# PEER stage of a hybrid encoder: one operand of VectorE's one-hots and sums moved into PSUM, gathered steps regrouped

## The reference

```python
q = (xt @ w_pq).reshape(T, 8, 2, 128)
s1 = einsum('thd,hnd->thn', q[:, :, 0], k1)      # 128 keys each
s2 = einsum('thd,hnd->thn', q[:, :, 1], k2)
t1, i1 = top_k(s1, 16); t2, i2 = top_k(s2, 16)
ts, ci = top_k(t1[..., :, None] + t2[..., None, :], 16)
e = i1[ci // 16] * 128 + i2[ci % 16]              # one of 16384 experts
g = softmax(ts)
act = gelu(einsum('td,thkd->thk', xt, u_tab[e]))
out = einsum('thk,thkd->td', g * act, v_tab[e])
```

## Time and profile before

| | us |
|---|---|
| median of 3 runs | 2577.13 |
| lowest, highest | 2574.62, 2577.2 |
| the profiled execution's own time | 2580.62 |
| its span, from first to last instruction | 2578.8 |

### The profile page before, as it was taken

The page is one execution under the profiler, slowest core; times in us unless marked ns, Lnnn a source line. Parts: engine busy times, 40 slices in busy tenths (PEclk is TensorE's granted clock), DMA queues, the critical chain, the costliest instruction groups (busy, mean ns, idle before and its releaser), DMA issues.

```text
span 2578.8 us, 29605 instructions
## 1 busy us (share of the span) xinstructions
PE 2331.2 (90%) x11005; PEld 1786.0 (69%) x11005; DVE 1622.4 (63%) x2696; ACT 666.8 (26%) x1419; POOL 964.2 (37%) x552
## 2 busy tenths in 40 slices
PE   6699999899879999997897988888879999999996
PEld 6699977665457978997897888888834444444442
DVE  2376654444543222999889799999835555555555
ACT  2143520133322212242333344434300110001011
POOL 8455455400004424264656665555411111111110
PEclk9899999955689999998998999999989999999998
DMA  6323233300133213164666777777799999999994
GB/s 237 105 99 109 98 107 124 104 20 17 33 94 139 66 33 128 42 233 139 226 229 203 235 252 282 281 271 280 268 361 371 374 381 378 386 377 383 383 376 180
DMA packets 192546, 541.94 MB, mean 210 GB/s; under 512 B 17057, under 2 KB 116194, under 8 KB 158882
## 3 DMA queue, kind: packets, MB, share of 16 engines
q1 hardware_dynamic: 113024, 243.30, 27.5%
q0 software_dynamic: 27776, 201.40, 20.4%
q10 hardware_dynamic: 51618, 95.52, 10.3%
HBM read 472.18 MB, written 67.67 MB: 209 GB/s over the span
## 4 chain that ended last, share of the span: by engine, by line
PE 61%; DVE 27%; issue 5%; ACT 2%; DMA 2%; POOL 2%; SPq 1%; ACTq 0%; DVEq 0%; POOLq 0%
PE ps L949 24%; PE ps L579 17%; PE ps L904 6%; PE ps L696 5%; DVE yg L1887 3%; PE ps L729 3%; DVE hot L2030 3%; DVE ring L1879 2%; DVE hot L2032 2%; PE ps L558 2%; PE ps L779 2%; PE ps L733 1%; DMA ge<-ge_scratch 1%; SPq L446 1%; DVE xn L1529 1%
## 5 line engine op out<-in xcount | busy, mean ns | idle before, releaser
L949 PE MATMUL ps<-vraw,gf 128*128 128x512 f32 x1536 | 665.1, 596 | 19.0 <-DVE gf L2046 11.4
L949 PEld LDWEIGHTS ps<-vraw,gf 128*128 128x128 f32 x1536 | 293.0, 191 | 390.6 <-issue 372.6
L505 POOL DMA_INDIRECT ring<-uv,place_of x192 | 228.0, 1188 | 789.6 <-DVE yg L1887 783.1
L904 PE MATMUL ps<-actH,uH 128*128 128x384 f32 x1024 | 355.7, 347 | 57.9 <-POOL uL L497 45.5
L497 POOL TENSOR_TENSOR uL<-uraw,uH 128x1024 fp32r<-128x1024 f32 x128 | 332.6, 2616 | 100.6 <-ACT uH L1389 99.3
L487 POOL TENSOR_SCALAR wH<-raw 128x1024 fp32r<-128x1024 f32 x112 | 120.5, 1094 | 653.7 <-PE ps L579 500.7
L904 PE MATMUL ps<-actL,uH 128*128 128x384 f32 x1024 | 349.1, 341 | 0.0
L904 PE MATMUL ps<-actH,uL 128*128 128x384 f32 x1024 | 348.4, 340 | 0.0
L1887 DVE SCALAR_TENSOR_TENSOR yg<-ring,coef,yg 128x1024 f32<-128x1024 f32 x192 | 280.0, 1458 | 36.6 <-ACT coef L1442 36.5
L1879 DVE SCALAR_TENSOR_TENSOR ring<-ring,xn 128x1024 f32<-128x1024 f32 x192 | 267.5, 1394 | 43.4 <-DMA ring<-uv,place_of 42.7
L579 PE MATMUL ps<-actH,wH 128*128 128x288 f32 (+1 forms) x960 | 288.2, 300 | 6.8 <-DVE actL L1546 6.8
(11 more groups left out here) (286 smaller groups left out, 3298.2 us busy)
## 6 DMA issues: line engine op xcount, KB each, us to landing
uraw<-wu SPq DMA_DIRECT2D x128, 512.0 KB, 4.4
vraw<-wv SPq DMA_DIRECT2D x128, 512.0 KB, 7.9
raw<-wts SPq DMA_DIRECT2D x56, 1024.0 KB, 4.9
ge_scratch<-ge ACTq DMA_DIRECT2D x128, 192.0 KB, 4.2
c_scratch<-cst ACTq DMA_DIRECT2D x12, 2048.0 KB, 8.1
cg<-c_scratch SPq DMA_DIRECT2D x32, 768.0 KB, 13.5
ge<-ge_scratch SPq DMA_DIRECT2D x128, 192.0 KB, 8.7
xres<-x ACTq DMA_DIRECT2D x2, 2048.0 KB, 12.1
```

The costliest lines, as they stand in the source:

```text
L505: pool.indirect_dma_start(out=ring[:, s % RING, :], out_offset=None, in_=a["uv"], in_offset=bass.IndirectOffsetOnAxis(ap=place_of[:, s:s + ...
L904: mm = pe.matmul(bank(b, TD), lhs, rhs, start=k == 0 and w == 0, stop=k == KT - 1 and w == 2)
L949: mm = pe.matmul(bank(2 * i + half), gf[:, q % GF_RING, i * P:(i + 1) * P], vraw[:, q % V_RING, half * CHUNK:(half + 1) * CHUNK], start=q ...
```

## The change

- **PSUM operands.** ACT copies iota into PSUM (`iota_ps`, bank 3) and the transposed gates stay there as `gates_ps` (bank 3), where PE's transposes put them; chosenT keeps only the two keys. So each of the three one-hot instructions has one operand in SBUF and one in PSUM. Tile 4's sums (`yg4`) lie in banks 4 and 5 during the up stage; ACT copies them to yg[:, 0] once the 64 accumulates are done, and PE's first down waits before it writes those banks (`yg4_copied`). The one-hots' products have three banks (C_BANKS) instead of four.
- **Steps.** All 64 early steps, which are those of tile 4, stand behind the 48 groups, hot_of_step(s) = s * 48 // 64; none in the ranking. `accumulate(s - 2)` follows `dot(s)` (LAG = 2), in the up stage and in the down stage. `gather(s)` is issued behind the `low` that is four ups after the group of step s - 2. ACT's coefficients of a group's steps stand before the copy_gates of the next group.
- **Places.** GATES_AT 13 to 16, EXPD_AT 54 to 42, TURN_AT 60 to 48, EXP3_AT 78 to 56, HOT_AT 75 to 54: the groups are spread over 73 ups instead of 52.

```diff
-PICKS_AT, GATES_AT, EXP4_AT, EXPD_AT, TURN_AT, EXP3_AT, HOT_AT, HOT_TO = 5, 13, 5, 54, 60, 78, 75, 127
-RANK_STEPS = 8
-RANKED = 3 * RANK_STEPS
-EARLY_STEPS = 64
+PICKS_AT, GATES_AT, EXP4_AT, EXPD_AT, TURN_AT, EXP3_AT, HOT_AT, HOT_TO = 5, 16, 5, 42, 48, 56, 54, 127
+EARLY_STEPS = STEPS4
+LAG = 2
...
 def hot_of_step(s):
-    return (s - RANKED) * HOTS // (EARLY_STEPS - RANKED)
+    return s * HOTS // EARLY_STEPS
...
-    chosenT = nc.alloc_sbuf_tensor_at("chosenT", [P, 3, TD], F32, offset=chosen_at)
+    chosenT = nc.alloc_sbuf_tensor_at("chosenT", [P, 2, TD], F32, offset=chosen_at)
...
+    iota_ps = ps[:, 3 * BANK + TD:4 * BANK]
+    gates_ps = ps[:, 3 * BANK:3 * BANK + TD]
+    yg4 = ps[:, 4 * BANK:6 * BANK]
+    C_BANKS = 3
...
-            while issued >= RING and step_place(issued - RING) + 4 <= n:
+            while RING <= issued < EARLY_STEPS and hot_place(hot_of_step(issued - LAG)) // 2 + 4 <= n:
                 gather(issued)
                 issued += 1
...
                 for s in range(3):
-                    mm = pe.transpose(ps[:, i * BANK + s * P:i * BANK + (s + 1) * P], chosen[:, i, s, :], ident[:, :])
+                    at = i * BANK + s * P if s < 2 else 3 * BANK + i * P
+                    mm = pe.transpose(ps[:, at:at + P], chosen[:, i, s, :], ident[:, :])
...
-                if q >= 4:
-                    pe.wait_ge(c_copied, q - 3)
+                if q >= C_BANKS:
+                    pe.wait_ge(c_copied, q - C_BANKS + 1)
...
+                if q == 0 and i == DENSE - 1:
+                    pe.wait_ge(yg4_copied, 1)
...
+            act.wait_ge(iota_in, 16)
+            act.activation(iota_ps, iota[:, :], ACT.Copy).then_inc(iota_copied, 1)
...
                     if hot_place(g) == h:
+                        for s in range(EARLY_STEPS):
+                            if hot_of_step(s) == g - 1:
+                                coefficient(s)
                         copy_gates(g)
-                        for s in range(RANKED, EARLY_STEPS):
-                            if hot_of_step(s) == g:
-                                coefficient(s)
...
+        act.wait_ge(acc_done, EARLY_STEPS)
+        act.activation(yg[:, 0, :], yg4, ACT.Copy).then_inc(yg4_copied, 1)
...
-            ve.scalar_tensor_tensor(yg[:, y_at, :], ring[:, s % RING, D:2 * D], coef[:, s:s + 1], yg[:, y_at, :],
-                                    ALU.mult, ALU.add).then_inc(acc_done, 1)
+            y = yg4 if s < STEPS4 else yg[:, 1, :]
+            ve.scalar_tensor_tensor(y, ring[:, s % RING, D:2 * D], coef[:, s:s + 1], y, ALU.mult, ALU.add)\
+              .then_inc(acc_done, 1)
...
-            dot(steps[0])
-            if steps[0]:
-                accumulate(steps[0] - 1)
+            s = steps[0]
+            if s < STEPS:
+                dot(s)
+            if s >= LAG:
+                accumulate(s - LAG)
...
-            rank(i, 0, PK_HEADS, full_work, gathered)
+            rank(i, 0, PK_HEADS, full_work, nothing)
...
-            ve.tensor_tensor(hot1[:, g % 2], iota[:, :].unsqueeze(1).broadcast_to(shape),
+            ve.tensor_tensor(hot1[:, g % 2], iota_ps.unsqueeze(1).broadcast_to(shape),
                              chosenT[:, 0, now].unsqueeze(2).broadcast_to(shape), ALU.is_equal)
-            step.done(ve.tensor_tensor(hot2[:, g % 2], iota[:, :].unsqueeze(1).broadcast_to(shape),
+            step.done(ve.tensor_tensor(hot2[:, g % 2], iota_ps.unsqueeze(1).broadcast_to(shape),
                                        chosenT[:, 1, now].unsqueeze(2).broadcast_to(shape), ALU.is_equal))
             ve.tensor_tensor(hot2[:, g % 2], hot2[:, g % 2],
-                             chosenT[:, 2, now].unsqueeze(2).broadcast_to(shape), ALU.mult).then_inc(hot_ready, 1)
+                             gates_ps[:, now].unsqueeze(2).broadcast_to(shape), ALU.mult).then_inc(hot_ready, 1)
...
+        while steps[0] < EARLY_STEPS + LAG:
+            accumulate(steps[0] - LAG)
+            steps[0] += 1
+        steps[0] = EARLY_STEPS
         for q in range(NKEYS):
             weigh(q)
             if steps[0] < STEPS:
-                gathered()
-        accumulate(STEPS - 1)
+                dot(steps[0])
+            if steps[0] >= EARLY_STEPS + LAG:
+                accumulate(steps[0] - LAG)
+            steps[0] += 1
+        for s in range(steps[0] - LAG, STEPS):
+            accumulate(s)
```

More of the change, by code:

```diff
@@ L388, in encoder_layer @@
         dot_ready acted_ready coef_ready acc_done gates_ready tile3_ready fold_ready folded
-        x2_in y_ready taken_up ss_in""".split()
+        x2_in y_ready taken_up ss_in iota_copied yg4_copied""".split()
     (const_in, gain_in, gain_used, memx_in, x_in, ssq_clear, ssq_ready, var_ready, std_ready, xn_ready, acth_done,
@@ L397, in encoder_layer @@
      dot_ready, acted_ready, coef_ready, acc_done, gates_ready, tile3_ready, fold_ready, folded,
-     x2_in, y_ready, taken_up, ss_in) = [S(name) for name in names]
+     x2_in, y_ready, taken_up, ss_in, iota_copied, yg4_copied) = [S(name) for name in names]
     ck_in = [S(f"ck_in{j}") for j in range(2)]
@@ L922, in c_tokens @@
                 q = 2 * g + half
-                if q >= 4:
-                    pe.wait_ge(c_copied, q - 3)
+                if q >= C_BANKS:
+                    pe.wait_ge(c_copied, q - C_BANKS + 1)
                 for t in range(4):
-                    at = (q % 4) * BANK + t * P
+                    at = (q % C_BANKS) * BANK + t * P
                     mm = pe.matmul(ps[:, at:at + P], hot1[:, g % 2, 4 * half + t, :], hot2[:, g % 2, 4 * half + t, :],
@@ L1414, in copy_choices @@
             act.wait_ge(chT_ready, DENSE)
+            act.wait_ge(iota_in, 16)
+            act.activation(iota_ps, iota[:, :], ACT.Copy).then_inc(iota_copied, 1)
             for i in range(DENSE):
                 act.activation(chosenT[:, :, i * P:(i + 1) * P],
-                               ps[:, i * BANK:i * BANK + 3 * P].rearrange("p (s t) -> p s t", s=3),
+                               ps[:, i * BANK:i * BANK + 2 * P].rearrange("p (s t) -> p s t", s=2),
                                ACT.Copy).then_inc(chT_copied, 1)
@@ L1428, in copy_gates @@
                 act.activation(cst[s][:, :, at + 4 * half:at + 4 * half + 4],
-                               bank(q % 4).rearrange("p (t e) -> p e t", t=4), ACT.Copy).then_inc(c_copied, 1)
+                               bank(q % C_BANKS).rearrange("p (t e) -> p e t", t=4), ACT.Copy).then_inc(c_copied, 1)
             if g % 4 == 3:
@@ L1464, in _ @@
                 exps(2 + DENSE, chosen[:, DENSE, 2, :])
-            for s in range(RANKED):
-                if step_place(s) + 1 == n:
-                    coefficient(s)
+        for s in range(EARLY_STEPS):
+            if hot_of_step(s) == HOTS - 1:
+                coefficient(s)
+        act.wait_ge(acc_done, EARLY_STEPS)
+        act.activation(yg[:, 0, :], yg4, ACT.Copy).then_inc(yg4_copied, 1)
         for s in range(EARLY_STEPS, STEPS):
@@ L1868, in best_of @@
             step.done(ins)
-        def row_of(s):
-            return (0, 0) if s < STEPS4 else (1, 1)
         def dot(s):
@@ L1876, in dot @@
                 ve.wait_ge(rows_in, 16)
-            x_at, _ = row_of(s)
+            x_at = 0 if s < STEPS4 else 1
             row = ring[:, s % RING, 0:D]
@@ L1993, in _ @@
         ve.sem_inc(gates_ready, 1)
-        step.done(ve.memset(yg[:, :, :], 0.0))
+        ve.memset(yg4, 0.0)
+        step.done(ve.memset(yg[:, 1, :], 0.0))
         step.done(ve.tensor_tensor(fold[:, :], ident[:, 0:NS_TOK], ident[:, NS_TOK:P], ALU.add))
@@ L2007, in _, with gates_at_first @@
         turn = [0]
-        def gathered_and_gates():
+        def gates_at_first():
             if turn[0] == 0:
@@ L2012, in gathered_and_gates @@
             turn[0] += 1
-            gathered()
         ve.wait_ge(ss_in, 16)
-        rank(DENSE, 0, PK_HEADS, full_work, gathered_and_gates)
+        rank(DENSE, 0, PK_HEADS, full_work, gates_at_first)
         expert_places(3, place_of[:, STEPS4:STEPS])
@@ L2020, in _ @@
         ve.wait_ge(chT_copied, DENSE)
+        ve.wait_ge(iota_copied, 1)
         for g in range(HOTS):
```

1 line of the change is left out of this document (removed).

## The result

The changed kernel takes **2619.51 us** (median of 4 runs, 2618.52 to 2624.7), the kernel before took 2577.16 beside it (2574.62 to 2577.28): ratio 1.0171, 95% interval 1.0153 to 1.0188. By that ratio it is 44 us slower (42 between the two medians); I had forecast +3. The profiled spans, 2622.9 and 2578.8, differ by 44.1 as well.

What follows compares the result with a forecast made beforehand. DVE was taken to bound the one-hot stage and PE the down stage. The terms, -3 to the end of the up stage and +6 in the down stage, gave +3 on 2580.6: 2584 us, or 2581 beside the median; range 2535 to 2620.

Steps and rivals of the forecast that it cites:

- rival 3: Down stage becomes bound by gathers, slots freed one step later: 2610 at landings of 8.2 us, 2668 at 9.1; chance 0.08.
- First one-hot: End of the ranking stage: 24 gathered steps leave it, 1482 - 126 = 1356 us, with 8 us either way.
- PSUM operands: DVE's one-hots and accumulates: no wait for POOL; accumulate that reads and writes PSUM taken at 1.2 us, 2.4 at most.
- Rival 4: One PSUM operand still waits for POOL, or writing PSUM is dear: +45 us, kernel 2625; chance 0.04.
- One-hot stage: First one-hot to end of up stage: chain of gathers makes it 513 us against 390 before, ending at 1869.
- landing: Gathers in the one-hot stage: median 6.7 us, 0.7 off for shorter issue, 1.2 on for long ones, 7.2.
- The third group and the clock's loss: One-hot stage, cycle of three groups: 8.1 us for the third group plus 2 us for PE's clock, sum 31.6.
- Clock: One-hot stage: behind waits of 4 to 5 us PE's clock is granted at 1.2 GHz, costing 2 us a cycle.
- Down stage: Sums two behind free a gather's slot one step later: +6 us, between 0 and 90, near the lower end.
- at 7.7 the loop is even: Down stage: with landings of 7.7 us, two steps hold landing, dot and accumulate within the 10.3 us PE needs.
- what was to show it: Signs: one-hots near 1.2 us, L927 waiting some 90, up stage ending near 1870, PE busy throughout the down stage.
- The issue row: Issue of gathers on POOL in the one-hot stage: 1.69 us of a landing, 0.95 at the shortest; 0.7 taken off.

Runs made afterwards that it cites:

- e8: The kernel before with the sums of the down stage two steps behind instead of one: 2607.24 us, ratio 1.0098.
- e1: The kernel before with the PSUM operands and sums and three banks alone, schedule as before: 2502.64 us, ratio 0.9709 to the kernel before.
- e2: The changed kernel with operands of one-hots and sums back in SBUF, its schedule kept: 2656.14 us, ratio 1.0319 to the kernel before.

## Why the prediction was wrong

What it said of the up stage held: the one-hot stage gives back what the ranking stage gains, because one-hots stand behind gathers and PE waits for them. In the down stage it was not the forecast that came true but its rival 3, which had a chance of 0.08. Two terms of the sum were too small: the one-hot stage by 25 us (513, 538) and the down stage by 28 (+6, +34), the larger part of the 41 us between +3 and +44.

- **First one-hot**: 1356 forecast, 1344.9 measured. 11 us in its favour, a little outside the 8 allowed. 7 of the 11 are not of the change: the ranking's first instruction starts at 1015.0 instead of 1022.3, and it started at 1016.4 in e8 too, whose program up to there is that of the kernel before. From it to the first one-hot 459.7 us became 329.8: 130 less, where 126 were forecast. The gathered steps account for 124 of them, 87 of work and 37 of waits. The ranking's own instructions came out 7 us shorter (325.6 to 318.7), within the 8 that the prediction allowed: L1934's 16.2 us became 2.9 (L1939) and L1917's 15.0 became 3.5 (L1922), while L1959's six went from 13.8 to 24.2 (L1964).
- **PSUM operands**: 1.2 us taken, 1.22 and 1.28 measured. Rival 4 is out.
- **One-hot stage**: 513 forecast, 538 measured. For 15 of the 16 gathers that are placed one group ahead and whose wait reached PE (the first, which landed in 12.4 us, left out) the traces give step by step: group to issue 7.60 us (forecast 7.6); landing **9.14** (7.2); dot, accumulate, three one-hots 6.1 (6.7); from group to group 22.9 (21.5). The third group and the clock's loss, 8.1 + 2.0 forecast, came to 10.4, as a cycle of three groups takes 33.3 us in the mean of the whole stage. So 33.3 x 47/3 = 522 instead of 495; this and not the shape of the chain is the 25 us. The step that failed is "median 6.7 in this stage ..., and I take 0.7 off ..., and 1.2 on for the long ones: 7.2". The 6.7 + 1.2 was right, for before the change the gathers of this stage landed in 7.9 us on average; and so was the 0.7, since their mean issue fell from 1.70 to 1.06 us. What I took as fixed was the rest of the landing, behind the issue. It grew from 6.2 to 7.1 us over the stage, and to about 8 for the 15 that matter. The 2 MB stores of the gates are a part of a long landing but not of the growth: before the change the 15 gathers of this stage that were in flight together with such a store (by over half a us) landed in 10.2 us on average and the other 25 in 6.5; after it 25 landed in 9.7 and the other 38 in 7.4. The share of the first kind stayed as it was, and it is the others that grew.
- **Clock**: some 2 us a cycle forecast; PE was busy 429 us for work that I had put at 393, 36 us over 15.7 cycles: 2.3. The rows bear it out: the one-hot matmuls took 120.9 us where e1's, at the full granted clock, took 93.4, and the ups some 8 more than at e1's means.
- **Down stage**: +6 forecast between bounds of 0 and 90, +34 measured. The formula (landing + 2.6)/2 - 5.15 a step came out right: with the landing of 8.24 us measured there it gives 0.27 x 128 = 35. The step that failed is "at 7.7 the loop is even", taken with "near the lower end". Landings did come down from 9.1 with two in flight, as argued, but to 8.2 and not to 7.7. The prediction named 8.2 and its price, 32 us, in rival 3, and gave it 0.08. It had taken DVE's 237 us of waits for gelus as a cushion. They were one only until the loop of slots became the longer one of the two; from there on every further microsecond of a step is PE's.

So -3 became +10 (+18 counted from the ranking's first instruction), +6 became +34, and 2619.5 lay just inside the range, half a us from its end. Of what was to show it, L2030, L2032, L2034 and L1887 near 1.2 us held, L927 waited (119.6 us, forecast some 90), and the up stage ended at 1883. But L927's waits stood before 17 of the 48 groups, one in three and not two, since of two gathers in a row that are placed one group ahead mostly only the first one's wait reached PE. PE was *not* busy throughout the down stage, and DVE's waits for gathered rows there were 310 us, not 100 to 250.

As to the Trainium skill, "SBUF — State Buffer": its figures of 620 and 3100 ns (section "A bandwidth-pool intuition that's wrong (but worth ruling out)") are of a DVE `tensor_copy`, which none of these instructions is. The issue row goes the same way (1.70 to 1.06 us as DVE gives way), but 0.64 us is a quarter of the 2.5 that I had estimated by them, and landings as a whole did not shorten. e2 beside the changed kernel shows what of it the operands alone do in one schedule: issues of 1.53 and 1.05 us, landings of 8.2 us in both.

## What to carry to other kernels

When an engine is relieved, ask what it waits for next before moving work onto it: here the operands alone were worth 2.9%, and the schedule built on them gave back more. For a buffer ring, count the time from the event that frees a slot, or allows an issue, to the use of what it brings, and price it with landings of the new order as well as of the old, since here those that mattered took 9.1 us, against a mean of 7.9 before and the 7.2 that I had allowed; where a term hangs on a threshold within that spread, take its middle and not the end that is hoped for. A change of two parts that cancel looks like no effect, so try each alone.

## What the runs showed of the hardware

- A DVE instruction of 128 x 1024 fp32 with one operand in PSUM takes as long as with both in SBUF and nothing in its way (1.22 and 1.21 us), and one that reads and writes PSUM 1283 ns, against 1279 to 1281 for SBUF sums in the down stage of these kernels. I had taken no surcharge and allowed for up to twice the time.
- With few two-SBUF instructions on DVE the issue of indirect DMAs on POOL (1.70 to 1.06 us) and `low` (2725 to 2490 ns) are shorter; between e2 and the changed kernel, where only the operands differ, they go from 1.53 to 1.05 us and from 2621 to 2490 ns. But the landings of 1 MB gathers went from 7.9 to 8.2 us on average, at about the same DMA share (0.75 and 0.71). The 15 whose wait reached PE landed in 9.1. Gathers in flight together with a 2 MB store took longer (10.2 against 6.5 us before the change); what the others queue behind, and why they grew to 7.4, was not tried and stays open.
